# The last down projection of a hybrid decoder layer: half of its operand tiles for all tokens, the other half for two groups of 256 tokens

## The chip, the cores and the metric

The kernel runs on one core of one Trainium2 chip. Its time is the device time of one execution in microseconds (us); lower is better. One core has a matrix engine (TensorE, PE in the profile), a vector engine (VectorE, DVE), a scalar engine (ScalarE, ACT), a general engine (GpSimd, POOL) and a queue for transfers (SyncE, SP). They run side by side, each through its own list of instructions in order, and wait for each other by semaphores. Data lies in SBUF (128 partitions); matrix products arrive in PSUM, in banks of 512 float32 per partition.

## What is computed

One decoder layer over 16 meta tokens and 512 tokens, model width 2048: a norm, an input projection, a short convolution beside a recurrent group, an output projection with residual, then the part that matters here, a norm, a squared-ReLU MLP with residual, and the final norm:

```python
    h = rms_norm(h_res, norm_mlp_g[i])
    h_res = h_res + jnp.square(jax.nn.relu(h @ w_up[i])) @ w_down[i]
out = rms_norm(h_res, final_norm_g)          # over the 2048 features of a token
return out[:, N_META:]                       # 512 tokens x 2048, float32
```

`w_up` is 2048 x 8192, `w_down` 8192 x 2048.

## The kernel before

Everything is held feature by token: 2048 features are 16 tiles of 128 partitions (`KT` = 16), the 512 tokens (`SEQ`) are the columns. The MLP goes in 8 groups (`FFG`) of 1024 hidden features. In a group the **up stage** makes 8 tiles of hidden features (`UT` = 8; `u_hi`, `u_lo`), and the **down stage** makes 16 output tiles, each a sum over these 8 operand tiles, that are added to the residual `res`. Groups 0 to 6 are one loop; the last group is written out, since the final norm goes on in its down stage.

**Precision.** Each product is three matmuls in the type fp32r: high weight by high data, high by low, low by high (`dense`, the function with the matmuls at L1491). So one output tile over 8 operand tiles is 24 matmuls of 512 columns.

**Weights.** They come in quarters: four 128 x 128 blocks (256 KB) by one transfer that SP issues (`load`, L442) into one of 4 buffers `w_raw`. ACT makes the high part `w_hi` (`split`, L745) and DVE the low part `w_lo` (L1045), both in rings of 8 quarters. SP's next load into a buffer waits for DVE's `lo_split` of the quarter four earlier, ACT's split waits for the landing and for PE's use of the quarter eight earlier (`quarter_used`), DVE's split waits for ACT's (`hi_split`), and PE waits for `lo_split`. A down tile takes two quarters.

**PSUM.** Output tile n goes to one of two banks of `PD` by turns; PE begins tile n when tile n-2 has been taken out (`evacuated`). DVE takes a down tile out by adding it to `res` (L1397).

**The end of the last group**, output tile m by output tile m. DVE: add m, then two splits. ACT: multiply tile m of `res` by the final gain into `nt1` (L978, semaphore `gained`), two splits, and copy the turned tile m-1 from PSUM into `rows` (`keep_rows`, L987). PE: after the matmuls of tile m, turn tile m-1 to token by feature, four 128 x 128 transposes into `PW` (`turn_out`, L1760). POOL: square tile m of `res` into `psq` (L689) and add it into `acc` (L691), in a loop of two tiles per pass for tiles 0 to 13, tile 14 written out; DVE squares tile 15 itself (L1404). After the last tile PE sums the squares per token (L1775: for each of 4 blocks of 128 tokens a matmul with `acc` and one with `sq_last`, one column each), ACT takes the square root (L993), DVE the reciprocal (L1406), and ACT (L997) and DVE (L1410) scale each its half of the columns of `rows`, block by block; SP stores 8 pieces of 512 KB (L513).

Each engine's order is that of the code; nothing is reordered by a planner.

Of the kernel before, what the change touches and what calls it, by code (L numbers as in the profile page):

```python
# [31 lines left out]
P = 128  # L32
# [29 lines left out]
KQ = 4  # L62
# [130 lines left out]
T_END = T_MLP + FFG * 24  # L193
# [3 lines left out]
def hybrid_layer(nc, x, meta, norm_mix_g, w_in, shift_mu, conv_w, decay_w0, decay_w2, iclr_a0, iclr_a2,  # L197
# [224 lines left out]
    T_LAST = T_MLP + 24 * (FFG - 1) + UT  # L422

# [4 lines left out]
    def _(sp):  # L428
# [90 lines left out]
    def _(pool):  # L519
# [178 lines left out]
        squares(T_OUT, 0, False)  # L698
        squares(T_LAST, ACC_STEPS, True)
# [5 lines left out]
    def _(act):  # L705
# [246 lines left out]
        def mlp_group(g, last=False):  # L952
            n_split = [0]

            def splits(count):
                for _ in range(count):
                    if n_split[0] < 64 - (EDGE_LEAD + 4 if last else 0):
                        split(Q_MLP + EDGE_LEAD + 4 + n_split[0], 64, g)
                    n_split[0] += 1
# [13 lines left out]
            for m in range(KT):  # L973

                act.wait_ge(evacuated[(T_LAST + m) % 2], free(T_LAST + m))
                if m >= 3:
                    act.wait_ge(fin_turned, m - 2)
                nc.scalar.activation(nt1[:, m % 3, :], res[:, m, :], ACT.Copy, scale=p_("g_fin", m)).then_inc(gained, 1)  # L978
                splits(2)
                if m:  # L980
                    keep_rows(m - 1)
            keep_rows(KT - 1)

        def keep_rows(m):

            act.wait_ge(fin_turned, m + 1)
            nc.scalar.copy(rows[:, :, m * P:(m + 1) * P], PW[:, m % 4, :].rearrange("p (t n) -> p t n", t=4)).then_inc(fin_kept, 1)  # L987
# [4 lines left out]
        act.wait_ge(summed, 2)  # L992
        nc.scalar.activation(rs_tok[:], PW[:, 0, 0:4], ACT.Sqrt, bias=eps_t[:, 0:1], scale=1.0 / D).then_inc(rooted, 1)  # L993
        act.wait_ge(rs_ready, 2)
        for t in range(4):
            r = rows[:, t, DH:D]
            nc.scalar.activation(r, r, ACT.Copy, scale=rs_tok[:, t:t + 1]).then_inc(rows_scaled[1], 1)  # L997
# [3 lines left out]
    def _(dve):  # L1001
# [364 lines left out]
        def mlp_group(g, last=False):  # L1366
            n_split = [0]

            def splits(count):
                for _ in range(count):  # L1370
                    if n_split[0] < 64 - (EDGE_LEAD + 4 if last else 0):
# [17 lines left out]
            for m in range(UT):  # L1389
# [3 lines left out]
                splits(3)  # L1393
            for m in range(KT):
# [3 lines left out]
                splits(2)  # L1398
# [4 lines left out]
        dve.wait_ge(evacuated[(T_END - 1) % 2], free(T_END - 1))  # L1403
        V.tensor_tensor(sq_last[:], res[:, KT - 1, :], res[:, KT - 1, :], ALU.mult).then_inc(last_squared, 1)  # L1404
        dve.wait_ge(rooted, 2)
        V.reciprocal(rs_tok[:], rs_tok[:]).then_inc(rs_ready, 1)  # L1406
        dve.wait_ge(rs_ready, 2)
        dve.wait_ge(fin_kept, KT)
        for t in range(4):
            V.tensor_scalar(rows[:, t, 0:DH], rows[:, t, 0:DH], rs_tok[:, t:t + 1], None, ALU.mult).then_inc(rows_scaled[0], 1)  # L1410
# [3 lines left out]
    def _(pe):  # L1414
# [58 lines left out]
        def dense(tiles, ktiles, q0, n0, hi, lo, per_q=0, per_n=0, it=0, operand=None, one_bank=range(0), first=0, spare=0, cut=()):  # L1473
# [3 lines left out]
            for t in range(tiles):  # L1477
# [3 lines left out]
                for k in range(ktiles):  # L1481
# [6 lines left out]
                    for i, (w, v) in enumerate(((whi, hi), (whi, lo), (wlo, hi))):  # L1488
                        begin, end = (k == 0 and i == 0), (k == ktiles - 1 and i == 2)
                        if t in one_bank:  # L1490
                            ins = M(pd_seq(n), w, v[:, k, first:first + SEQ], start=begin, stop=end)  # L1491
# [262 lines left out]
        def turn_out(m):  # L1754

            pe.wait_ge(gained, m + 1)
            if m >= 4:
                pe.wait_ge(fin_kept, m - 3)
            for t in range(4):
                ins = nc.tensor.transpose(PW[:, m % 4, t * P:(t + 1) * P],  # L1760
                                          nt1[:, m % 3, t * P:(t + 1) * P], ident[:])
            ins.then_inc(fin_turned, 1)

        pe.wait_ge(rooted, 1)
        for i, _ in enumerate(down(FFG - 1), 1):
            if i % UT == 0 and i > UT:
                turn_out(i // UT - 2)

        pe.wait_ge(acc_step, 2 * ACC_STEPS)
        pe.wait_ge(fin_kept, KT - 3)  # L1770
        turn_out(KT - 1)
        pe.wait_ge(last_squared, 2)
        for t in range(4):
            for i, squares in enumerate((acc, sq_last)):
                ins = M(PW[:, 0, t:t + 1], squares[:, t * P:(t + 1) * P], ones[:, 0:1], start=(i == 0),  # L1775
                        stop=(i == 1))
        ins.then_inc(summed, 1)
# [29 lines left out]
```

## Time and profile before

| | |
|---|---|
| median of 3 runs | 2438.83 us (2438.52 to 2440.35) |
| profiled execution | 2439.01 us, of it span in the trace 2437.2 us |
| PE busy | 2406.8 us, 99% |
| DVE busy | 1129.1 us, 46% |
| ACT busy | 781.7 us, 32% |
| POOL busy | 193.8 us, 8% |
| down stage of the last group | 2324.0 to 2419.6 us of the span |
| from its last matmul to the end | 2419.6 to 2437.2 us |

The profiled execution stands 0.18 us over the median. Busy shares are means over the whole program; a stage is read from its own rows. "Idle before <-X" in a row is the time that the engine stood idle ahead of it, and what released it. The span is the time in the trace; 1.8 us of the device time lie outside it.

### The profile page before, as it was taken

The numbers are of one execution on the slowest core, as the hardware profiler recorded it, in microseconds if no ns is written. First come the engines' busy times: TensorE is split into PE (matmuls) and PEld (weight loads), VectorE is DVE, ScalarE is ACT, GpSimd is POOL, SyncE is SP. The second block draws the span as 40 slices with busy tenths as digits, with TensorE's granted clock in tenths as the row PEclk, the third lists the DMA queues.
The fourth block names the chain that finished last, engine by engine and source line by source line (L and its number), as shares of the span: only waits on it lengthen the run. The fifth ranks groups of instructions, "written<-read, shape, count | busy, mean of one in ns | idle before, by whom it ended". The sixth has DMA issues, their size and how long they took to land.

```text
span 2437.2 us, 42098 instructions
## 1 busy us (share of the span) xinstructions
PE 2406.8 (99%) x16524; PEld 2033.6 (83%) x16524; DVE 1129.1 (46%) x1733; ACT 781.7 (32%) x1321; POOL 193.8 (8%) x240
## 2 busy tenths in 40 slices
PE   8999999999999999999999999999999999999997
PEld 8999998999998788888888788888788887888886
DVE  7557657657657543533233333333333333333353
ACT  6533434434434322432232222221221322222333
POOL 5001101001001222000000000000000000000032
PEclk9999999999999999999999999999999999999998
DMA  8344244244244632333333233333332332333332
GB/s 246 81 98 102 69 100 98 71 102 99 73 104 108 192 103 82 100 98 93 87 104 95 81 110 94 88 97 94 87 104 87 91 108 79 104 98 91 89 99 92
DMA packets 487453, 243.65 MB, mean 100 GB/s; under 512 B 83295, under 2 KB 481121, under 8 KB 486881
## 3 DMA queue, kind: packets, MB, share of 16 engines
q1 hardware_dynamic: 480560, 222.62, 33.1%
q0 software_dynamic: 6720, 18.45, 2.4%
q8 instruction: 144, 2.36, 0.4%
q14 instruction: 29, 0.23, 0.0%
HBM read 224.08 MB, written 16.92 MB: 99 GB/s over the span
## 4 chain that ended last, share of the span: by engine, by line
PE 85%; DVE 9%; DMA 3%; ACT 1%; issue 1%; SPq 1%; ACTq 0%; DVEq 0%
PE PD L1491 66%; PE PD L1496 10%; PE PD L1705 2%; DVE w_lo L1045 1%; DVE uni L1140 1%; DVE uni L1266 1%; DMA w_raw<-in_w_in 1%; PE PD L1520 1%; PE PW L1520 1%; DMA UU<-gram 1%; DMA gram<-NA 1%; PE PW L1667 1%; PE PD L1425 0%; DVE uni L1144 0%; ACT w_hi L745 0%
## 5 line engine op out<-in xcount | busy, mean ns | idle before, releaser
L1045 DVE TENSOR_TENSOR w_lo<-w_raw,w_hi 128x512 fp32r<-128x512 f32 x780 | 544.2, 730 | 302.5 <-ACT w_hi L745 299.1
L745 ACT CAST w_hi<-w_raw 128x512 fp32r<-128x512 f32 x780 | 456.8, 618 | 702.7 <-PE PD L1491 519.9
L1491 PE MATMUL PD<-act_lo,w_hi 128*128 128x512 f32 x1344 | 531.3, 395 | 0.0
L1491 PE MATMUL PD<-act_hi,w_hi 128*128 128x512 f32 x1344 | 529.7, 394 | 1.5 <-DVE res L1338 1.5
L1491 PE MATMUL PD<-act_hi,w_lo 128*128 128x512 f32 x1344 | 528.7, 393 | 1.1 <-issue 1.1
L1491 PE MATMUL PD<-u_hi,w_hi 128*128 128x512 f32 x1024 | 409.7, 400 | 0.0
L1491 PE MATMUL PD<-u_hi,w_lo 128*128 128x512 f32 x1024 | 403.3, 394 | 0.0
L1491 PE MATMUL PD<-u_lo,w_hi 128*128 128x512 f32 x1024 | 401.5, 392 | 0.0
L1491 PEld LDWEIGHTS PD<-act_hi,w_hi 128*128 128x128 f32 x1344 | 252.4, 188 | 66.7 <-issue 4.8
L1491 PEld LDWEIGHTS PD<-act_hi,w_lo 128*128 128x128 f32 x1344 | 252.8, 188 | 57.2
L1491 PEld LDWEIGHTS PD<-act_lo,w_hi 128*128 128x128 f32 x1344 | 252.1, 188 | 58.0 <-issue 0.2
L1397 DVE TENSOR_TENSOR res<-PD,res 128x512 f32<-128x512 f32 x128 | 88.5, 692 | 407.7 <-PE PD L1491 407.7
L1496 PE MATMUL PD<-act_hi,w_hi 128*128 128x264 f32 (+1 forms) x1248 | 266.7, 295 | 0.0
L1496 PE MATMUL PD<-act_lo,w_hi 128*128 128x264 f32 (+1 forms) x1248 | 251.3, 283 | 0.0
L1496 PE MATMUL PD<-act_hi,w_lo 128*128 128x264 f32 (+1 forms) x1248 | 251.2, 283 | 0.0
L1491 PEld LDWEIGHTS PD<-u_hi,w_lo 128*128 128x128 f32 x1024 | 192.2, 188 | 49.9
L1491 PEld LDWEIGHTS PD<-u_lo,w_hi 128*128 128x128 f32 x1024 | 192.3, 188 | 45.4
L1491 PEld LDWEIGHTS PD<-u_hi,w_hi 128*128 128x128 f32 x1024 | 192.2, 188 | 43.6
L1381 DVE SCALAR_TENSOR_TENSOR nt<-PD,rs 128x512 f32<-128x512 f32 x64 | 44.3, 692 | 369.1 <-PE PD L1491 368.8
L965 ACT ACTIVATE nt<-nt 128x512 f32<-128x512 f32 x64 | 40.5, 633 | 515.6 <-DVE nt L1381 515.6
L1496 PEld LDWEIGHTS PD<-act_hi,w_hi 128*128 128x128 f32 x1248 | 192.6, 189 | 11.8 <-issue 6.7
L1496 PEld LDWEIGHTS PD<-act_hi,w_lo 128*128 128x128 f32 x1248 | 192.2, 188 | 0.0
(314 smaller groups left out, 1867.0 us busy)
## 6 DMA issues: line engine op xcount, KB each, us to landing
w_raw<-in_w_up SPq DMA_DIRECT2D x256, 256.0 KB, 3.2
w_raw<-in_w_down SPq DMA_DIRECT2D x256, 256.0 KB, 3.0
w_raw<-in_w_in SPq DMA_DIRECT2D x200, 256.0 KB, 3.2
w_raw<-in_w_out SPq DMA_DIRECT2D x64, 256.0 KB, 2.8
residual<-res POOLq DMA_DIRECT2D x2, 2048.0 KB, 9.9
out<-rows SPq DMA_DIRECT2D x8, 512.0 KB, 4.9
uni<-inverse SPq DMA_DIRECT2D x16, 240.0 KB, 4.0
yin<-mixed POOLq DMA_DIRECT2D x15, 256.0 KB, 3.8
```

Of the source, the lines that this page charges most:

```text
L745: nc.scalar.copy(w_hi[:, q % RING], w_raw[:, q % RAW]).then_inc(hi_split, 1)
L965: nc.scalar.activation(nt, nt, ACT.Square).then_inc(u_sq, 1)
L1045: V.tensor_tensor(w_lo[:, q % RING], w_raw[:, q % RAW], w_hi[:, q % RING].bitcast(F32), ALU.subtract).then_inc(lo_split, 1)
L1140: done("inv", V.reciprocal(fsq, fsq))
L1266: done("inv2", V.reciprocal(ysq, ysq))
L1381: V.scalar_tensor_tensor(nt1[:, m % 3, :], pd_seq(n), 0.0, rs1[:], ALU.max, ALU.mult).then_inc(evacuated[n % 2], 1)
L1397: V.tensor_tensor(res[:, m, :], pd_seq(n), res[:, m, :], ALU.add).then_inc(evacuated[n % 2], 1)
L1491: ins = M(pd_seq(n), w, v[:, k, first:first + SEQ], start=begin, stop=end)
L1496: ins = M(PD[:, 2 * (n % 2) + a, cols], w, v[:, k, start:start + cols.stop - cols.start], start=begin, stop=end)
L1520: ins = M(bank[:, h, cols], w, v[:, k, start:start + cols.stop - cols.start], start=begin, stop=end)
L1667: ins = M(PW[:, (c - 1) % 2, 0:P], GT[:, c - 1, :], HB[:, 0, :] if c == 1 else ZB[:, c - 2, :], start=True, stop=True)
L1705: ins = M(PD[:, OUT_BANK[t], :], w, v[:, k, 0:SEQ], start=(k == 0 and i == 0), stop=(k == KT - 1 and i == 2))
```

## The change

Only the down stage of the last group and what follows it. The first four operand tiles (the first quarter of each output tile) are multiplied for all 512 tokens, 16 output tiles of 12 matmuls with 512 columns, and added to `res` (**part one**). The last four operand tiles are multiplied for tokens 0 to 255, 16 tiles, and then for tokens 256 to 511, 16 tiles more (**part two**, 32 steps i = 0 to 31, 12 matmuls of 256 columns each). The quarters of part two are loaded and split once for each half. At every step of part two the gain, the turn (two transposes) and the copy to `rows` go over 256 tokens. At step 17 the squares of the first half are summed, rooted and inverted, at steps 19 and 20 its two blocks are scaled, and SP stores them. The same for the second half stands at the end. POOL's squares are written out, 15 tiles of 256 columns for each half, in part two only; DVE squares tile 15 of each half.

```diff
+        for m in range(KT):
+            load(wdn_q[FFG - 1, 0, :, :, m, :], Q_LAST + m)
+        for i in range(2 * KT):
+            load(wdn_q[FFG - 1, 1, :, :, i % KT, :], Q_HALF + i)
...
+        for h in range(2):                                   # POOL
+            cols = slice(h * NEAR, (h + 1) * NEAR)
+            for m in range(KT - 1):
+                n = T_HALF + h * KT + m
+                pool.wait_ge(evacuated[n % 2], free(n))
+                pool.wait_ge(acc_step, steps)
+                nc.gpsimd.tensor_tensor(psq[:, cols], res[:, m, cols], res[:, m, cols], ALU.mult).then_inc(acc_step, 1)
+                pool.wait_ge(acc_step, steps + 1)
+                nc.gpsimd.tensor_tensor(acc[:, cols], acc[:, cols], psq[:, cols], ALU.add).then_inc(acc_step, 1)
...
+            splits(KT)                                       # ACT
+            for i in range(2 * KT):
+                h, m = divmod(i, KT)
+                act.wait_ge(evacuated[(T_HALF + i) % 2], free(T_HALF + i))
+                if i >= 3:
+                    act.wait_ge(fin_turned, i - 2)
+                nc.scalar.activation(nt1[:, i % 3, 0:NEAR], res[:, m, h * NEAR:(h + 1) * NEAR], ACT.Copy,
+                                     scale=p_("g_fin", m)).then_inc(gained, 1)
+                splits(1)
+                if i:
+                    keep_rows(i - 1)
+                if i == SUM_AT:
+                    root_tokens(0)
+                if i in SCALE_AT:
+                    scale_rows(SCALE_AT.index(i))
...
             for m in range(KT):                              # DVE
-                n = T_MLP + UT + m
-                dve.wait_ge(quarter_used, at(Q_MLP + 4 * UT + 2 * (m + 1), 64, g))
+                n = T_LAST + m
+                dve.wait_ge(quarter_used, Q_LAST + m + 1)
                 V.tensor_tensor(res[:, m, :], pd_seq(n), res[:, m, :], ALU.add).then_inc(evacuated[n % 2], 1)
-                splits(2)
+                splits(1)
+            for i in range(2 * KT):
+                h, m = divmod(i, KT)
+                n, cols = T_HALF + i, slice(h * NEAR, (h + 1) * NEAR)
+                dve.wait_ge(quarter_used, Q_HALF + i + 1)
+                dve.wait_ge(evacuated[(T_LAST + m) % 2], free(T_LAST + m))
+                V.tensor_tensor(res[:, m, cols], pd_seq(n)[:, 0:NEAR], res[:, m, cols], ALU.add).then_inc(evacuated[n % 2], 1)
+                if m == KT - 1:
+                    dve.wait_ge(evacuated[n % 2], free(n))
+                    V.tensor_tensor(sq_last[:, cols], res[:, m, cols], res[:, m, cols], ALU.mult).then_inc(last_squared, 1)
+                splits(1)
+                if i == SUM_AT:
+                    invert_tokens(0)
+                if i in SCALE_AT:
+                    scale_rows(SCALE_AT.index(i))
...
+        for _ in dense(KT, KQ, Q_LAST, T_LAST, u_hi, u_lo, operand=operand, one_bank=range(KT)):   # PE
+            pass
+        pe.wait_ge(u_ready, UT * FFG)
+        for h in range(2):
+            near = dense(KT, KQ, Q_HALF + KT * h, T_HALF + KT * h, u_hi[:, KQ:UT], u_lo[:, KQ:UT], first=h * NEAR, width=NEAR,
+                         one_bank=range(KT))
+            for step_, _ in enumerate(near, 1):
+                i = KT * h + step_ // KQ - 1
+                if step_ % KQ == 0 and i:
+                    turn_out(i - 1)
+                if step_ % KQ == 0 and i == SUM_AT:
+                    sum_tokens(0)
+
+        turn_out(2 * KT - 1)
+        sum_tokens(1)
```

`splits` in the last group now covers 72 quarters after the first 8 instead of 56: 32 in the up stage, 16 in part one, one at each of the steps 0 to 23 of part two.

How instructions stand in a row, first on DVE where the up stage goes over into the down stage, before:

```order
L1381 SCALAR_TENSOR_TENSOR nt<-PD,rs 128x512 [waits u_ready,quarter_used]
L1045 TENSOR_TENSOR w_lo<-w_raw,w_hi 128x512 [waits hi_split]
L1386 TENSOR_TENSOR u_lo<-nt,u_hi 128x512 [waits u_hi_ready]
L1045 TENSOR_TENSOR w_lo<-w_raw,w_hi 128x512 [waits hi_split] x3
L1397 TENSOR_TENSOR res<-PD,res 128x512 [waits quarter_used]
L1045 TENSOR_TENSOR w_lo<-w_raw,w_hi 128x512 [waits hi_split] x2
```

and in the changed kernel on DVE where part one goes over into part two (L1442 is the add of part one, L1449 that of part two, L1083 the split):

```order
L1442 TENSOR_TENSOR res<-PD,res 128x512 [waits quarter_used]
L1083 TENSOR_TENSOR w_lo<-w_raw,w_hi 128x512 [waits hi_split]
L1449 TENSOR_TENSOR res<-PD,res 128x256 [waits evacuated1,quarter_used]
L1083 TENSOR_TENSOR w_lo<-w_raw,w_hi 128x512 [waits hi_split]
L1449 TENSOR_TENSOR res<-PD,res 128x256 [waits evacuated0,quarter_used]
```

A tile had two splits behind its add; now every add of 256 columns has one split behind it and one ahead.

ACT in the last group's down stage before (`nt1` is the gained tile, `rows` the copy of the turned one):

```order
L987 COPY rows<-PW 128x4x128 [waits fin_turned]
L978 ACTIVATE nt1<-res,par 128x512 [waits fin_turned,evacuated1]
L745 CAST w_hi<-w_raw 128x512 [waits quarter_used,raw_loaded0]
L745 CAST w_hi<-w_raw 128x512 [waits quarter_used,raw_loaded1]
L987 COPY rows<-PW 128x4x128 [waits fin_turned]
```

and in part two of the changed kernel:

```order
L1001 ACTIVATE nt1<-res,par 128x256 [waits fin_turned,evacuated1]
L767 CAST w_hi<-w_raw 128x512 [waits quarter_used,raw_loaded0]
L1016 COPY rows<-PW 128x2x128 [waits fin_turned]
L1001 ACTIVATE nt1<-res,par 128x256 [waits fin_turned,evacuated0]
L767 CAST w_hi<-w_raw 128x512 [waits quarter_used,raw_loaded1]
```

The gain still stands ahead of the split, at half the width; the split has its full width, and there is one for each gain.

POOL where the squares of the last group begin, before (ISA and REGISTER_ALU rows are waits and address arithmetic of the loop):

```order
L683 MEMSET acc 128x512 [waits summed]
L693 UNCONDITIONAL_BRANCH
L693 ISA
L688 ISA [waits evacuated1]
L689 ISA [waits acc_step]
L689 TENSOR_TENSOR psq<-res 128x512
L690 REGISTER_ALU
L691 TENSOR_TENSOR acc<-acc,psq 128x512 [waits acc_step]
```

and in the changed kernel:

```order
L710 MEMSET acc 128x512 [waits summed]
L718 TENSOR_TENSOR psq<-res 128x256 [waits acc_step,evacuated1]
L720 TENSOR_TENSOR acc<-acc,psq 128x256 [waits acc_step]
L718 TENSOR_TENSOR psq<-res 128x256 [waits acc_step,evacuated0]
L720 TENSOR_TENSOR acc<-acc,psq 128x256 [waits acc_step]
```

The loop and its arithmetic are gone, and the pair of operations comes 30 times at half the width.

## Rows read from the trace of the kernel before

**Rows 1.** The page's first part: busy time, share, instructions.
```profile
PE 2406.8 (99%) x16524; PEld 2033.6 (83%) x16524; DVE 1129.1 (46%) x1733; ACT 781.7 (32%) x1321; POOL 193.8 (8%) x240
```
**Rows 2.** Chain that ended last, from 2380 us: start, length, what.
```profile
2413.55 0.44 PE PW L1760 x4
2413.99 5.61 PE PD L1491 x24
...
2419.62 0.70 DVE res L1397
...
2420.35 0.73 ACT nt L978
...
2421.33 0.63 PE PW L1760 x4
2421.95 1.78 PE PW L1775 x16
```
**Rows 3.** Timeline, DVE, up stage into down stage: start, length, line, idle before.
```profile
2323.96 0.69 DVE L1381 SCALAR_TENSOR_TENSOR nt<-PD,rs 128x512 f32<-128x512 f32 x1 [5.46 <-PE PD L1491]
...
2327.73 1.89 DVE L1045 TENSOR_TENSOR w_lo<-w_raw,w_hi 128x512 fp32r<-128x512 f32 x3
2329.56 0.69 DVE L1397 TENSOR_TENSOR res<-PD,res 128x512 f32<-128x512 f32 x1
...
2337.15 2.39 DVE L1045 TENSOR_TENSOR w_lo<-w_raw,w_hi 128x512 fp32r<-128x512 f32 x2 [1.30 <-ACT w_hi L745]
```
**Rows 4.** Timeline, ACT, one output tile of the last down stage.
```profile
2335.88 0.72 ACT L978 ACTIVATE nt<-res,par 128x512 f32<-128x512 f32 x1 [3.40 <-DVE res L1397]
2336.51 1.12 ACT L745 CAST w_hi<-w_raw 128x512 fp32r<-128x512 f32 x2
```
**Rows 5.** Timeline, PE, pairs of 260 and 256 columns: first and last of 26.
```profile
599.89 0.40 PE L1496 MATMUL PD<-act_hi,w_hi 128*128 128x260 f32 x2
...
605.84 0.40 PE L1496 MATMUL PD<-act_lo,w_hi 128*128 128x260 f32 x2
```
**Rows 6.** Timelines, DVE and then POOL, at three output tiles of the last stage.
```profile
2349.22 0.69 DVE L1045 TENSOR_TENSOR w_lo<-w_raw,w_hi 128x512 fp32r<-128x512 f32 x1 [1.30 <-ACT w_hi L745]
2349.83 1.78 DVE L1045 TENSOR_TENSOR w_lo<-w_raw,w_hi 128x512 fp32r<-128x512 f32 x1
...
2413.59 0.69 DVE L1397 TENSOR_TENSOR res<-PD,res 128x512 f32<-128x512 f32 x1 [5.34 <-PE PD L1491]
...
2336.12 1.04 POOL L689 TENSOR_TENSOR psq<-res 128x512 f32 x1 [2.66 <-DVE res L1397]
...
2349.30 1.75 POOL L691 TENSOR_TENSOR acc<-acc,psq 128x512 f32<-128x512 f32 x1
...
2414.36 1.04 POOL L689 TENSOR_TENSOR psq<-res 128x512 f32<-128x512 f32 x1 [3.44 <-DVE res L1397]
2415.48 1.29 POOL L691 TENSOR_TENSOR acc<-acc,psq 128x512 f32<-128x512 f32 x1
```
**Rows 7.** Groups by form (count, busy us, mean ns), then the scaling's timeline.
```profile
L1016 DVE COPY res<-PD 128x256 f32<-128x256 f32 x1 | 0.4, 425 | 4.2 <-PE PD L1446 4.2
...
L563 POOL TENSOR_TENSOR centre<-ident,head_mean 128x128 f32<-128x128 f32 x1 | 0.5, 458 | 0.1
...
2424.27 4.27 ACT L997 ACTIVATE rows<-rows,rs_tok 128x1024 f32<-128x1024 f32 x4 [0.24 <-DVE rs_tok L1406]
2424.27 2.74 DVE L1410 TENSOR_SCALAR rows<-rows,rs_tok 128x1024 f32<-128x1024 f32 x4
```
**Rows 8.** Windows in the last stores: five engines' busy time, granted clock, DMA share, GB/s.
```profile
2426.00:2426.50 0.50, 0.00 (x0) 0.00 (x0) 0.50 (x2) 0.50 (x2) 0.00 (x0) 0.50 1.02 410
...
2436.00:2436.50 0.50, 0.00 (x0) 0.00 (x0) 0.00 (x0) 0.00 (x0) 0.00 (x0) 0.50 0.58 221
```
**Rows 9.** Windows with the granted clock: near the program's start, and in its tail.
```profile
19.50:21.00 1.50, 0.57 (x5) 0.60 (x6) 0.84 (x3) 1.50 (x5) 0.21 (x2) 1.00 0.16 26
...
2423.00:2423.50 0.50, 0.50 (x6) 0.50 (x5) 0.00 (x0) 0.00 (x0) 0.00 (x0) 0.91 0.00 0
```

More of the change, by code:

```diff
@@ L420, in hybrid_layer @@
     RS_CUT = META + 3 * P
-    T_LAST = T_MLP + 24 * (FFG - 1) + UT
     block = ctx.enter_context(nc.Block())
@@ L956, in splits @@
                 for _ in range(count):
-                    if n_split[0] < 64 - (EDGE_LEAD + 4 if last else 0):
+                    if n_split[0] < (80 - EDGE_LEAD - 4 if last else 64):
                         split(Q_MLP + EDGE_LEAD + 4 + n_split[0], 64, g)
@@ L991, in _ @@
         mlp_group(FFG - 1, last=True)
[L992 to L997, printed above, removed]
+        root_tokens(1)
+        for t in range(2, 4):
+            scale_rows(t)
     @block.vector
@@ L1370, in splits @@
                 for _ in range(count):
-                    if n_split[0] < 64 - (EDGE_LEAD + 4 if last else 0):
+                    if n_split[0] < (80 - EDGE_LEAD - 4 if last else 64):
                         split(Q_MLP + EDGE_LEAD + 4 + n_split[0], 64, g)
@@ L1393, in mlp_group, with invert_tokens, scale_rows @@
                 splits(3)
+            if not last:
+                for m in range(KT):
+                    n = T_MLP + UT + m
+                    dve.wait_ge(quarter_used, at(Q_MLP + 4 * UT + 2 * (m + 1), 64, g))
+                    V.tensor_tensor(res[:, m, :], pd_seq(n), res[:, m, :], ALU.add).then_inc(evacuated[n % 2], 1)
+                    splits(2)
+                return
             for m in range(KT):
-                n = T_MLP + UT + m
-                dve.wait_ge(quarter_used, at(Q_MLP + 4 * UT + 2 * (m + 1), 64, g))
+                n = T_LAST + m
+                dve.wait_ge(quarter_used, Q_LAST + m + 1)
                 V.tensor_tensor(res[:, m, :], pd_seq(n), res[:, m, :], ALU.add).then_inc(evacuated[n % 2], 1)
-                splits(2)
+                splits(1)
+            for i in range(2 * KT):
+                h, m = divmod(i, KT)
+                n, cols = T_HALF + i, slice(h * NEAR, (h + 1) * NEAR)
[10 more added lines that the diff above has]
+                    scale_rows(SCALE_AT.index(i))
+        def invert_tokens(h):
+            dve.wait_ge(rooted, 2 + h)
+            r = rs_tok[:, 2 * h:2 * h + 2]
+            V.reciprocal(r, r).then_inc(rs_ready, 1)
+        def scale_rows(t):
+            dve.wait_ge(rs_ready, 2 + t // 2)
+            dve.wait_ge(fin_kept, KT * (t // 2 + 1))
+            V.tensor_scalar(rows[:, t, 0:DH], rows[:, t, 0:DH], rs_tok[:, t:t + 1], None, ALU.mult).then_inc(rows_scaled[0], 1)
         with dve.Fori(0, FFG - 1) as g:
@@ L1402, in _ @@
         mlp_group(FFG - 1, last=True)
[L1403 to L1410, printed above, removed]
+        invert_tokens(1)
+        for t in range(2, 4):
+            scale_rows(t)
     @block.tensor
@@ L1490, in dense @@
                         if t in one_bank:
-                            ins = M(pd_seq(n), w, v[:, k, first:first + SEQ], start=begin, stop=end)
+                            ins = M(pd_seq(n)[:, 0:width], w, v[:, k, first:first + width], start=begin, stop=end)
                             continue
@@ L1769, in _, with turn_out @@
[L1769 to L1777, printed above, removed]
+        def turn_out(i):
+            pe.wait_ge(gained, i + 1)
+            if i >= 4:
+                pe.wait_ge(fin_kept, i - 3)
+            for t in range(2):
+                ins = nc.tensor.transpose(PW[:, i % 4, t * P:(t + 1) * P],
+                                          nt1[:, i % 3, t * P:(t + 1) * P], ident[:])
+            ins.then_inc(fin_turned, 1)
@@ new lines, in sum_tokens @@
+        def sum_tokens(h):
+            pe.wait_ge(acc_step, ACC_STEPS + 1 + 2 * (KT - 1) * (h + 1))
+            pe.wait_ge(last_squared, 2 + h)
+            for t in range(2):
+                for i, squares in enumerate((acc, sq_last)):
+                    ins = M(PD[:, 1 + 2 * h, t:t + 1], squares[:, (2 * h + t) * P:(2 * h + t + 1) * P], ones[:, 0:1],
+                            start=(i == 0), stop=(i == 1))
+            ins.then_inc(summed, 1)
+        pe.wait_ge(rooted, 1)
+        operand = lambda k: pe.wait_ge(u_ready, UT * (FFG - 1) + k + 1)
```

61 lines of the change are left out of this document (32 added, 29 removed).

## The prediction, made before the changed kernel ran

> **What bounds the kernel now.** The page's first part says it: PE is busy 99% of the span, DVE and ACT are not [rows 1]. So time is won only where PE's work gets less or where PE has nothing to do. The chain that ended last shows both [rows 2]: in the last down stage 5.61 us of 24 matmuls (0.2335 us each) and 0.44 us of four transposes by turns, with nothing between; then from 2419.62, the end of the last matmul, 17.6 us to the end of the span at 2437.2 in which PE does almost nothing. The change goes for that tail. It pays in the stage ahead of it, where adds, gains, turns and splits, spread over 6.04 us per tile so far, have to fit into steps of about a quarter of that. So the timelines of DVE, ACT and POOL come next [rows 3, 4, 6]: what follows what, and how soon.
>
> **Part one.** The stage begins at 2323.96, where DVE takes out the last up tile [rows 3]. 16 tiles of 12 matmuls at 0.2335 are 44.8 us. One stall: the first add is due after 2.8 us, at 2326.8, but DVE stands in its splits until 2329.56 [rows 3]; tile 2 needs that bank, could start at 2329.56 and has it at 2330.25. That is 0.7 us. Afterwards an add (0.69) and a split (0.60, from the start spacing of three in 1.89 [rows 3]) fit into 2.8. Part two begins at 2323.96 + 44.8 + 0.7 = 2369.5.
>
> **Part two, PE's own work.** Pairs of 260 and 256 columns, each matmul with its weight load, start 5.95 us apart for 25 pairs [rows 5], 0.238 a pair, so 0.119 for 258 columns and 0.118 for 256: 1.42 us a step. The narrow matmuls cost next to nothing extra (1.42 against 1.40 for half of a 512-column tile of this depth). Two transposes are 0.22. If PE stayed the bound, part two would take 32 x 1.42 + 30 x 0.22 + 0.9 for the sum of the first half (8 of the 16 small matmuls that took 1.78 [rows 2]) = 52.9.
>
> **Part two, the ring of waits.** It doesn't stay the bound. At steps 0 to 23 the order tables show: DVE adds tile i, then splits a quarter, and that split waits for ACT's split of the same quarter; ACT makes its gain of tile i first, and that waits for DVE's add. So add i, gain i, high split, low split, add i+1 stand in one row. That ACT or DVE has idle time does not help, and PE can't run ahead by more than two banks. In numbers, from the start of an add:
> - add of 256 columns: 0.43, from 0.69 for 512 and the PSUM copies of DVE, 0.425 at 256 [rows 3, 7].
> - gain: starts 0.03 later [rows 2]. At 512 columns the split behind it starts 0.63 later [rows 4]; at 1024 columns such an operation repeats every (4.27 - 1.14)/3 = 1.04, with one of them at 1.14 long [rows 7], so 0.8 ns a column and 0.42 at 256. ACT's split starts at 0.88.
> - DVE's low split can start 0.64 after ACT's (2336.51 to 2337.15 [rows 3, 4]), at 1.52, and takes 0.60 to the next add: **2.13 us**, if nothing else is in the way.
>
> **And POOL is in the way.** It works at each step from 0 to 14 and 16 to 30 now. The rows show what that costs [rows 6]: with POOL's add into acc running from 2349.30 to 2351.05, DVE's second split lasts 1.78 in place of 0.69 and ends 0.56 after POOL's does; POOL's add took 1.75 in place of 1.29. POOL's own times: square 1.04 and add 1.29 at 512 columns alone, starting 0.08 after DVE's add (2414.28 to 2414.36) and 0.08 after each other [rows 6]; 0.458 at 128 columns [rows 7] gives a slope of 2.2 ns and 0.18 fixed, so 0.74 for the add at 256 and 0.61 for the square. From the start of DVE's add: square 0.51 to 1.12, add 1.20 to 1.94. DVE's split wants to start at 1.52, ends at 1.94 + 0.56 = 2.50, and the next add starts 0.08 earlier, since DVE's operations overlap by that much: **2.42 us** a step. I take this one, because POOL's add starts 0.32 before DVE asks. The bounds are 2.13 (DVE first, POOL after it) and 2.61 (POOL starts 0.27 after DVE's add ends, as in the loop before: ACT's gain starts at 2335.88, so the add ended at 2335.85, and POOL starts at 2336.12 [rows 4, 6]; the loop's arithmetic is gone now).
>
> The Trainium skill, page "SBUF — State Buffer", section "SBUF: two separate sides", says that VectorE with two SBUF inputs and a reading GpSimd operation exclude each other, the first one holding the port for its whole instruction. The trace agrees with it: 1.78, and an end 0.56 after POOL's. If they shared a rate instead (1.09 us lost in 1.22 us side by side), the 0.42 us of overlap here would cost 0.37, a step 2.50, and the sum below would come out 1.8 us higher.
>
> **The sum of part two.** Add 0 starts at 2369.5 + 1.42 + 0.02 = 2370.9. To add 23 there are 23 steps: 22 x 2.42, and step 15 with no POOL work at 2.13 (DVE's extra square of tile 15 hides while it waits for ACT), together 55.4. Step 17 adds 0.2 for the reciprocal (ACT's root is done by then: it comes at 1.7 to 2.0 in a step of 2.42). Steps 19 and 20 add DVE's scaling, 0.69 each [rows 7], since it stands between split and add; ACT's, 1.04, ends before its next gain. Together 57.0: add 23 at 2427.9. From step 24 there are no splits left and PE binds again. It still waits for gain 23 (0.98 after add 23) and 0.25 to start (2421.08, where the last gain ends, to 2421.33 [rows 2]), turns (0.22), does tile 25; the same once more behind gain 24; then five steps of 1.64: add 31 starts 2.42 + 0.98 + 0.25 + 0.22 + 1.42 + 5 x 1.64 = 13.5 later, at 2441.4. Before, the last add started at 2419.62: **21.8 us later**.
>
> **The tail.** Before, from the last add to the scaling 4.65 (2419.62 to 2424.27). After: add 0.43, gain 0.03 + 0.52, start 0.25, two transposes 0.32, sums 0.89, root and reciprocal 0.54 as before: 2.98, 1.67 less. POOL's last add ends 0.3 us after add 31 starts, under it. The stores then bind: 8 pieces, 4.19 MB, keep the transfers full from 2426.0 to 2436.3 at some 405 GB/s [rows 8]; four pieces take 5.15 instead of 10.3. ACT's second block is scaled 2.2 after the first begins, ahead of its transfer. Together the tail is **6.8 us shorter**.
>
> **Costs taken at nothing.** 16 more loads: SP's load for step i is released four steps (over 9 us) ahead, against about 3 us to land; cover is gone only if steps fall under 1 us. The stores of the first half stand behind all loads in SP's list, but the last load is released at step 19 and the first block is scaled there, so they run under steps 20 to 27. ACT's own work in a step (0.42 + 0.52 + 0.3) is 1.3, below the ring.
>
> **Total.** +21.8 - 6.8 = +15.0 on the profiled execution's 2439.0, so 2454.0; the median stands 0.2 lower: **2453.8 us**.
>
> **Rivals.**
> - *Ring without POOL* (12%): DVE's split gets in first. 22 x 0.29 less: 2447.4. For it: only 0.32 us decide, and POOL's times at 256 columns are estimates. Against: whoever asks first holds, and POOL asks first.
> - *Ring stretched* (6%): POOL starts late as in the loop, or overlap is shared: 2.50 to 2.61, 2455.6 to 2458.
> - *PE stays the bound, not slower* (3%): 52.9 for part two, add 31 at 2422.4, 2.8 later, less 6.8: 2434.8, just within 0.2%. It needs a ring below 1.64, and the change stops paying from a ring of about 1.77 on (15.0 / 23 below 2.42). The four links alone, with no semaphore between, are 0.43 + 0.42 + 0.62 + 0.60 = 2.07, so it would take a step of the ring that isn't one.
> - *The clock falls* (5%): in part two PE would stand idle 0.8 of 2.42 us. At 1.2 GHz, half of the granted 2.4, a step is 3.28 and PE binds: part two 106, up to 2488. Against: near the start PE was busy for 0.57 of 1.5 us at a granted clock of 1.00 [rows 9]; it fell to half only in the tail, where from 2420.0 on PE had stood idle 1.3 us and then did one-column matmuls (0.91 in the window of the change [rows 9]).
> - *The early stores don't run early* (2%): 5.15 more, 2459.
>
> **How the numbers follow.** The forecast (ring with POOL, 2450 to 2457) gets 72%, the rivals 12, 6, 3, 5 and 2. Range 2446 to 2460: it takes in both bounds of the ring, and 1 to 2 us for tail and transitions. A measurement here can tell about 0.2%, 4.9 us. Faster by more than that 0.01 (even the ideal gains 4.0), within it 0.04, slower 0.95.
>
> **What would show it.** In the trace of the changed kernel: adds of 256 columns 2.4 us apart at steps 0 to 14, about 2.1 at step 15, 3.1 at 19 and 20, 1.64 from step 26; DVE's splits lasting 0.9 to 1.0 beside POOL's add, and idle before "ACT w_hi"; PE idle 0.8 us in each step, waiting for the gain; part one 45.5 us; the last add near 2441, and 10.8 us from there to the end. Wrong it would be if adds were 1.64 apart (the ring isn't closed), 2.13 (no POOL in it) or 3.3 (the clock).

## The result, and the profile after

The changed kernel takes 2452.23 us (median of 5 runs, 2450.43 to 2453.43) against 2438.52 for the one before (5 runs beside them, 2438.14 to 2440.35): a ratio of 1.0057, interval 1.0046 to 1.0068. It is slower by 13.7 us; 15.0 were forecast (2453.8).

Both kernels do the same work up to the last down stage, but they reach it at different times: the last up tile is scaled at 2323.96 before [rows 3] and at 2323.17 after, and in the kernels of the experiments below anywhere from 2319.64 to 2323.69, although nothing ahead of it was changed in any of them. So the traces are compared below by the **stretch** from the start of that scaling to the end of the span: 113.24 us before, 127.33 after, 14.1 more. Each kernel was traced once, but the stretch repeats where kernels should not differ: the last add starts 116.87 us after the scaling here and in experiment 6, and 116.86 in experiment 5 with the added work outside the ring.

The first part of the page after, to be held against [rows 1]:

```profile
span 2450.5 us, 42509 instructions
PE 2413.4 (98%) x16716; PEld 2045.7 (83%) x16716; DVE 1146.0 (47%) x1783; ACT 797.8 (33%) x1370; POOL 195.1 (8%) x270
```

The timeline of DVE after (start us, us, engine, line, operation, out<-in, shape, count, idle before and what ended it). It answers to [rows 3] and [rows 6]:

```profile
2323.17 0.69 DVE L1419 SCALAR_TENSOR_TENSOR nt<-PD,rs 128x512 f32<-128x512 f32 x1 [5.45 <-PE PD L1555]
...
2370.43 0.43 DVE L1449 TENSOR_TENSOR res<-PD,res 128x256 f32<-128x256 f32 x1
2371.94 0.97 DVE L1083 TENSOR_TENSOR w_lo<-w_raw,w_hi 128x512 fp32r<-128x512 f32 x1 [1.09 <-ACT w_hi L767]
2372.84 0.41 DVE L1449 TENSOR_TENSOR res<-PD,res 128x256 f32<-128x256 f32 x1
2374.34 0.97 DVE L1083 TENSOR_TENSOR w_lo<-w_raw,w_hi 128x512 fp32r<-128x512 f32 x1 [1.08 <-ACT w_hi L767]
2375.23 0.41 DVE L1449 TENSOR_TENSOR res<-PD,res 128x256 f32<-128x256 f32 x1
...
2407.75 0.69 DVE L1083 TENSOR_TENSOR w_lo<-w_raw,w_hi 128x512 fp32r<-128x512 f32 x1 [0.63 <-ACT w_hi L767]
...
2415.59 0.41 DVE L1449 TENSOR_TENSOR res<-PD,res 128x256 f32<-128x256 f32 x1
2417.09 0.97 DVE L1083 TENSOR_TENSOR w_lo<-w_raw,w_hi 128x512 fp32r<-128x512 f32 x1 [1.08 <-ACT w_hi L767]
2417.98 0.74 DVE L1467 TENSOR_SCALAR rows<-rows,rs_tok 128x1024 f32<-128x1024 f32 x1
2418.64 0.41 DVE L1449 TENSOR_TENSOR res<-PD,res 128x256 f32<-128x256 f32 x1
```

And of ACT, and of POOL, in the same steps:

```profile
2373.29 0.51 ACT L1001 ACTIVATE nt<-res,par 128x256 f32<-128x256 f32 x1 [1.38 <-DVE res L1449]
2373.70 0.60 ACT L767 CAST w_hi<-w_raw 128x512 fp32r<-128x512 f32 x1
2374.21 0.36 ACT L1016 COPY rows<-PW 128x256 f32<-128x256 f32 x1
```

```profile
2373.33 0.61 POOL L718 TENSOR_TENSOR psq<-res 128x256 f32<-128x256 f32 x1 [0.96 <-DVE res L1449]
2374.02 0.73 POOL L720 TENSOR_TENSOR acc<-acc,psq 128x256 f32<-128x256 f32 x1
```

The ring of waits can be read off in one step, by start times: DVE's add 2372.84, ACT's gain 2373.29, ACT's high split 2373.70, DVE's low split 2374.34, next add 2375.23, which is 2.39 us after the first. POOL's add ends at 2374.75, and DVE's split, which began its record at 2374.34, ends 0.56 later and lasts 0.97. The split at 2407.75 is the control within the same trace: it stands in step 15, where POOL has no square or add, and it takes 0.69.

The waits between 2371 and 2428 (engine and line, what it waited for: us in total, times, longest):

```profile
ACT nt L1001 <- DVE res L1449: 25.6, 24, 1.4
DVE w_lo L1083 <- ACT w_hi L767: 25.6, 24, 1.1
...
PE PW L1824 <- ACT nt L1001: 12.1, 22, 1.2
```

DVE waits for ACT and ACT for DVE, the same 25.6 us each, and PE waits behind both: 0.55 us on average, 0.51 in a plain step and 1.17 and 1.18 behind the two scalings. After such a wait the two transposes last 0.44 us in place of 0.22, so a plain step loses 0.73 us against PE's own 1.655. The last steps and the tail, in the chain that ended last (start us, us, what; against [rows 2]):

```profile
2430.30 1.44 PE PD L1555 x12
2431.74 0.22 PE PW L1824 x2
...
2440.04 0.44 DVE res L1449
2440.48 0.02 issue
2440.50 0.52 ACT nt L1001
2441.02 0.04 issue
2441.06 0.44 PE PW L1824 x2
2441.50 0.80 PE PD L1833 x8
2442.30 0.02 issue
2442.32 0.27 ACT rs_tok L1021
2442.59 0.02 issue
2442.62 0.18 DVE rs_tok L1462
```

Three windows (stretch, its length, busy us and count of PE, PEld, DVE, ACT and POOL, granted clock, DMA share, GB/s):

```profile
2372.00:2384.00 12.00, 9.58 (x74) 8.56 (x73) 6.58 (x11) 6.32 (x15) 6.80 (x11) 1.00 0.38 109
2420.00:2422.00 2.00, 1.52 (x13) 1.32 (x12) 1.87 (x3) 1.42 (x3) 0.55 (x1) 1.00 1.07 417
2444.00:2448.00 4.00, 0.00 (x0) 0.00 (x0) 0.23 (x1) 1.01 (x1) 0.00 (x0) 0.50 0.91 364
```

The clock stayed at 1.00, its 2.4 GHz level, through the ring; the first half's rows are stored from 2420 on, under the second half's work (417 GB/s in the first two microseconds, the last load of weights among it); and the last four pieces leave in the tail.

### The profile page after: what moved, and what is told of

It reads as the page before. It is cut to its first block, busy times and chain, and to the rows that moved or that the text cites. A ratio compares the mean times of both kernels' runs of the same rounds, so it can differ in the third digit from the quotient of the medians.

```text
span 2450.5 us, 42509 instructions
## 1 busy us (share of the span) xinstructions
PE 2413.4 (98%) x16716; PEld 2045.7 (83%) x16716; DVE 1146.0 (47%) x1783; ACT 797.8 (33%) x1370; POOL 195.1 (8%) x270
## 3 DMA queue, kind: packets, MB, share of 16 engines
q8 instruction: 146, 2.39, 0.4%
## 4 chain that ended last, share of the span: by engine, by line
PE 86%; DVE 8%; issue 2%; ACT 2%; DMA 1%; SPq 0%; ACTq 0%; DVEq 0%
PE PD L1555 65%; PE PD L1560 12%; PE PD L1769 2%; DVE w_lo L1083 1%; DVE uni L1178 1%; DVE uni L1304 1%; PE PD L1584 1%; ACT w_hi L767 1%; PE PW L1584 1%; PE PW L1731 1%; DVE res L1449 0%; PE PD L1489 0%; DVE uni L1182 0%; PE PW L1695 0%; PE PW L1633 0%
## 5 line engine op out<-in xcount | busy, mean ns | idle before, releaser
L767 ACT CAST w_hi<-w_raw 128x512 fp32r<-128x512 f32 x796 | 468.0, 619 | 734.5 <-PE PD L1555 549.1
L1083 DVE TENSOR_TENSOR w_lo<-w_raw,w_hi 128x512 fp32r<-128x512 f32 x796 | 549.6, 721 | 314.1 <-ACT w_hi L767 310.5
L1555 PE MATMUL PD<-u_hi,w_hi 128*128 128x512 f32 (+1 forms) x1088 | 421.8, 388 | 0.8 <-DVE res L1442 0.8
L1555 PE MATMUL PD<-u_hi,w_lo 128*128 128x512 f32 (+1 forms) x1088 | 414.2, 381 | 0.0
L1555 PE MATMUL PD<-u_lo,w_hi 128*128 128x512 f32 (+1 forms) x1088 | 412.3, 379 | 0.0
L1436 DVE TENSOR_TENSOR res<-PD,res 128x512 f32<-128x512 f32 x112 | 77.5, 692 | 371.3 <-PE PD L1555 371.3
L1555 PEld LDWEIGHTS PD<-u_hi,w_lo 128*128 128x128 f32 x1088 | 204.2, 188 | 46.9
L1555 PEld LDWEIGHTS PD<-u_lo,w_hi 128*128 128x128 f32 x1088 | 204.6, 188 | 42.9
L1555 PEld LDWEIGHTS PD<-u_hi,w_hi 128*128 128x128 f32 x1088 | 204.3, 188 | 42.8 <-DVE res L1442 1.2
```

The source lines that it names most:

```text
L767: nc.scalar.copy(w_hi[:, q % RING], w_raw[:, q % RAW]).then_inc(hi_split, 1)
L1083: V.tensor_tensor(w_lo[:, q % RING], w_raw[:, q % RAW], w_hi[:, q % RING].bitcast(F32), ALU.subtract).then_inc(lo_split, 1)
L1555: ins = M(pd_seq(n)[:, 0:width], w, v[:, k, first:first + width], start=begin, stop=end)
```

## The experiments

The theory: the ring (add, gain, high split, low split) sets the step, and POOL's two operations lengthen its last link, because DVE's split does not run beside them. Its rivals: POOL does not matter; the length of ACT's work does, wherever it stands; it is not the order of operations but their amount. All edits below are made to the changed kernel and touch part two alone, if nothing else is said.

**1. The split ahead of the gain.** ACT's split needs nothing of this step's add; only the order of the lines puts it behind.

```diff
+                splits(1)
                 act.wait_ge(evacuated[(T_HALF + i) % 2], free(T_HALF + i))
...
                 nc.scalar.activation(nt1[:, i % 3, 0:NEAR], ...)
-                splits(1)
```

> The changed kernel with one edit: at each step of part two ACT makes the high split ahead of the gain, so the split waits for the matmuls of tile i and no longer for DVE's add. Theory (a ring add, gain, high split, low split): the ring is cut, steps 0 to 23 fall from 2.39 us toward PE's own 1.65, and 24 x 0.74 = 17.8 us come off at most. POOL (1.43 us a step) and DVE's split (0.6) then ask for the same time, 2.0 in 1.65, so POOL falls behind by 0.35 a step and the sums of each half wait 2 to 3 us for it: about 2439, between 2436 and 2442. Rival (steps are long because 256-column matmuls or the doubled loads are slow): the step stays near 2.39, time near 2452.

2438.47 us (10 runs), before beside it 2437.67 (19 runs), ratio 1.0003, interval 0.9994 to 1.0013: the whole loss is gone. The stretch is 113.3. So the ring was the loss, and ACT and DVE have the time for their work. But the shorter tail doesn't show as a gain either: the last add starts 102.47 after the scaling, 6.8 later than in the kernel before, and the tail is 6.8 shorter. Of the 6.8, 4.4 are there without POOL's work too (experiment 4: PE's narrow matmuls and the first half's sums, the stall in part one, two waits for a gain). The timelines of this kernel say where the rest went. DVE:

```profile
2371.58 0.96 DVE L1083 TENSOR_TENSOR w_lo<-w_raw,w_hi 128x512 fp32r<-128x512 f32 x1 [0.28 <-ACT w_hi L767]
...
2397.42 0.41 DVE L1449 TENSOR_TENSOR res<-PD,res 128x256 f32<-128x256 f32 x1
```

and POOL:

```profile
2372.08 1.07 POOL L720 TENSOR_TENSOR acc<-acc,psq 128x256 f32<-128x256 f32 x1
...
2394.99 0.88 POOL L718 TENSOR_TENSOR psq<-res 128x256 f32<-128x256 f32 x1
2395.94 1.01 POOL L720 TENSOR_TENSOR acc<-acc,psq 128x256 f32<-128x256 f32 x1
2397.09 0.88 POOL L718 TENSOR_TENSOR psq<-res 128x256 f32<-128x256 f32 x1
```

and its waits:

```profile
PE PD L1833 <- POOL acc L720: 2.1, 1, 2.1
```

POOL has no idle time ahead of any of these rows. Its pair (0.61 + 0.73) comes every 1.57 us where DVE has no split left, just under PE's 1.65 a step; beside DVE's splits it comes every 1.98 us on average over the first half's 15 pairs (2.10 in the rows shown), and POOL is the slowest engine. It falls behind, and PE waits 2.1 us for the first half's sums at step 17. In the chain that ended last POOL stands from 2391.0 to the end of its adds at 2427.6, where PE forms the last sums; that end costs 0.35 (10.82 from the last add to the end against 10.47 in experiment 4). DVE's adds are not touched: the one at 2397.42 lies wholly inside POOL's square (2397.09 to 2397.97) and takes 0.41. It has one operand in PSUM, the split has both in SBUF.

**2. POOL idle.** Its square and add in part two become one-column fills, with the same semaphores; the final norm lacks these squares.

```diff
-                nc.gpsimd.tensor_tensor(psq[:, cols], res[:, m, cols], res[:, m, cols], ALU.mult).then_inc(acc_step, 1)
+                nc.gpsimd.memset(psq[:, 0:1], 0.0).then_inc(acc_step, 1)
...
-                nc.gpsimd.tensor_tensor(acc[:, cols], acc[:, cols], psq[:, cols], ALU.add).then_inc(acc_step, 1)
+                nc.gpsimd.memset(psq[:, 0:1], 0.0).then_inc(acc_step, 1)
```

> The changed kernel, but in part two POOL's squares and adds are each replaced by a one-column memset (the final norm then lacks these squares). Order and semaphores stay. Theory: DVE's split no longer waits for POOL, it lasts 0.69 in place of 0.97, and the step falls from 2.39 to the four links alone, 2.11 to 2.13: 21 x 0.27 = 5.7 us less, about 2446.5. Rival (POOL's share is nothing, the split is long for another reason): step stays 2.39, 2452.

2446.4 us in one run, stretch 121.0, which is 6.3 less than after. Its timeline of DVE:

```profile
2373.08 0.42 DVE L1449 TENSOR_TENSOR res<-PD,res 128x256 f32<-128x256 f32 x1
2374.58 0.69 DVE L1083 TENSOR_TENSOR w_lo<-w_raw,w_hi 128x512 fp32r<-128x512 f32 x1 [1.09 <-ACT w_hi L767]
2375.19 0.42 DVE L1449 TENSOR_TENSOR res<-PD,res 128x256 f32<-128x256 f32 x1
```

The split is asked for at the same point of the step (1.50 after the add) and takes 0.69; the step is 2.11. POOL's part of the step is 0.28, the other links are 2.11.

**3. POOL busy with fills.** Is it POOL's activity, or what its operations do? First two fills of 512 columns for the square and the add (again without those squares), then three.

```diff
-                nc.gpsimd.tensor_tensor(psq[:, cols], res[:, m, cols], res[:, m, cols], ALU.mult).then_inc(acc_step, 1)
+                nc.gpsimd.memset(psq[:], 0.0).then_inc(acc_step, 1)
...
-                nc.gpsimd.tensor_tensor(acc[:, cols], acc[:, cols], psq[:, cols], ALU.add).then_inc(acc_step, 1)
+                nc.gpsimd.memset(psq[:], 0.0).then_inc(acc_step, 1)
```

> The changed kernel, but in part two POOL's two operations are memsets of 512 columns (0.53 us each in the trace of before): POOL is as busy at the time of DVE's split, 1.2 to 1.7 us into a step, and writes SBUF, but reads nothing (the final norm then lacks these squares). Theory that DVE's two-source split and POOL exclude each other by their reads: step 2.11 to 2.13 as with POOL idle, about 2446.5. Rival (any work of POOL on SBUF holds DVE up): split of 0.8 to 0.9, step 2.2 to 2.4, 2448 to 2452.

2442.8 us in one run; the stretch is 121.0 as with POOL idle (the time is lower because this execution reached the stage 3.6 us earlier). But the run decides little: the second fill ran from 2374.75 to 2375.27 and DVE's split started at 2375.20, so they were side by side for 0.07 us only. Hence a third fill, ahead of the last:

```diff
+                nc.gpsimd.memset(act_lo[:, m, :].bitcast(mybir.dt.float32), 0.0)
                 nc.gpsimd.memset(psq[:], 0.0).then_inc(acc_step, 1)
```

> GpSimd's square and add of each step of the last four operand tiles are replaced by three fills of 512 columns each (0.52 us each beside the gaps of 0.06 in the earlier run with two fills), so that GpSimd is at work from about 0.48 to 2.2 us after the start of VectorE's add, over the whole of VectorE's weight split (asked for at 1.50, 0.69 long). The final norm lacks these squares. Theory A, only GpSimd's operations on two tensors shut VectorE's split out: the step stays at 2.11 us and the split at 0.69, and from the last scaling to the end of the span 121.0 us pass, as with two fills. Rival B, any work of GpSimd on its memory port shuts VectorE's split out: the split ends some 0.56 us behind the last fill, that is at 2.8 rather than 2.19, the step grows to about 2.7 us (0.6 more, over 24 steps), and the stretch to about 135 us.

2445.06 us in one run, stretch 121.25. Its rows of DVE and of POOL:

```profile
2375.07 0.69 DVE L1084 TENSOR_TENSOR w_lo<-w_raw,w_hi 128x512 fp32r<-128x512 f32 x1 [1.08 <-ACT w_hi L768]
...
2377.18 0.69 DVE L1084 TENSOR_TENSOR w_lo<-w_raw,w_hi 128x512 fp32r<-128x512 f32 x1 [1.09 <-ACT w_hi L768]
```

```profile
2374.62 0.54 POOL L720 MEMSET act_lo<- 128x528 f32 x1
2375.10 0.53 POOL L721 MEMSET psq<- 128x512 f32 x1
```

Now the fill from 2375.10 to 2375.63 lies wholly inside the split from 2375.07 to 2375.76, and neither is longer than alone; steps stay 2.11 apart. The stretch is 0.2 longer than in experiment 2 behind the last add alone; up to that add 110.54 and 110.52 us pass. So what shuts the split out is not POOL at work but its add, which unlike a fill reads SBUF.

**4. The first two together**: split first and POOL idle, to see what the change is worth where nothing binds but PE.

> Both edits: split ahead of the gain, and POOL's squares in part two replaced by one-column memsets (the final norm lacks these squares). Theory: PE binds all of part two at 1.65 a step, part two takes 53 us, and the time is what the prediction gave for PE as the bound, 2434.8, about 4 below the kernel before. Rival (something else holds a step over 1.65, such as landings of the doubled loads, or PSUM's two banks): steps of 1.8 and more, 2438 or above.

2434.73 us (10 runs), ratio 0.999, interval 0.9981 to 1.0. The stretch is 110.6, 2.7 below before, adds 1.65 apart. This is what the forecast's third rival, "PE stays the bound", described, and it is near its price: 2.7 by the stretch (2.9 by the medians) in place of 4.0. The rows of DVE show steps in which DVE waits for PE, with all doubled loads and narrow matmuls in place, so neither of these sets the step:

```profile
2373.34 0.42 DVE L1449 TENSOR_TENSOR res<-PD,res 128x256 f32<-128x256 f32 x1 [0.25 <-PE PD L1555]
...
2374.99 0.42 DVE L1449 TENSOR_TENSOR res<-PD,res 128x256 f32<-128x256 f32 x1 [0.26 <-PE PD L1555]
```

**5. More work of ACT inside the ring, and outside it.** A second gain of 256 columns into a buffer that nobody reads: between gain and split, or behind the copy of the rows.

```diff
                 nc.scalar.activation(nt1[:, i % 3, 0:NEAR], ...)
+                nc.scalar.activation(act_lo[:, m, h * NEAR:(h + 1) * NEAR], res[:, m, h * NEAR:(h + 1) * NEAR], ACT.Copy, scale=p_("g_fin", m))
                 splits(1)
                 if i:
                     keep_rows(i - 1)
```

> The changed kernel with one more ACT operation of 256 columns at each step of part two (the gain once more, into a place that nobody reads), between gain and split. Theory (ring of four links, POOL's add beside it): ACT's split comes 0.42 later, DVE's split asks at 1.92 instead of 1.50, when POOL's add (it ends 1.93 after the add's start) is over, so the step is the bare ring plus 0.42 = 2.53, 0.14 over 2.39, and DVE's split lasts 0.69 again. From the last up tile's scaling to the end 127.3 + 23 x 0.14 = 130.5. If POOL had no part in the step: 2.39 + 0.42 = 2.81, 137. If the ring isn't what binds: 127.3.

> The same extra ACT operation, but behind the copy to rows, so outside the ring. Theory: ACT has 1.1 us free in a step of 2.39, the step stays 2.39, and the stretch from the last up tile's scaling to the end stays 127.3. Rival (ACT is simply too full): step 2.39 + 0.42, 137.

Inside: one run, 2453.84 us, stretch 130.57, adds 2.51 apart:

```profile
2371.32 0.42 DVE L1450 TENSOR_TENSOR res<-PD,res 128x256 f32<-128x256 f32 x1
2373.22 0.69 DVE L1084 TENSOR_TENSOR w_lo<-w_raw,w_hi 128x512 fp32r<-128x512 f32 x1 [1.48 <-ACT w_hi L767]
2373.83 0.42 DVE L1450 TENSOR_TENSOR res<-PD,res 128x256 f32<-128x256 f32 x1
```

The operation delays the split by 0.40, and the step grows only by 0.12: DVE now asks at 1.90, just as POOL's add ends, and its split is back at 0.69. That is the ring of the forecast's lower bound, DVE's split untouched by POOL, with 0.40 more in it, and one run sizes the two terms (0.40 more of ACT, 0.28 less of POOL). Outside: one run, 2449.94 us, stretch 127.3, steps of 2.39, nothing. The same work costs 3.2 us or none by its place in the list.

**6. The stores held back.** SP waits for three scaled blocks before it stores the first.

```diff
-                sp.wait_ge(rows_scaled[h], t + 1)
+                sp.wait_ge(rows_scaled[h], max(t + 1, 3))
```

> The changed kernel, with one edit: SP waits with the stores of the first half until the first block of the second half is scaled, so all eight pieces leave at the end. Theory (the last 10.46 us are short because only four pieces of 512 KB are left): the stretch up to the last add stays 116.9, and the tail grows by four pieces at some 405 GB/s, 5.2 us, to 15.6; from the last up tile's scaling to the end 132.5. Rival (the tail is shorter because of sums and scaling, the stores overlap anyway): 127.3 to 129.

2454.68 us in one run, stretch 132.6. The last add starts 116.87 after the scaling, exactly as in the changed kernel, and from there to the end it takes 15.72 in place of 10.46: 5.26 more, for the four pieces that were put at 5.15. Transfers run at 404 to 406 GB/s from 2442 to 2452. So the early stores bring what was reckoned, and cost the work that they run under nothing that shows.

**7. A version without ring and without POOL's squares.** The split goes first, and DVE makes each square right behind its add (0.42 us, of which it has enough), so that POOL only adds.

```diff
+                    V.tensor_tensor(squares_of[:, m, cols], res[:, m, cols], res[:, m, cols], ALU.mult).then_inc(squared, 1)
...
-                nc.gpsimd.tensor_tensor(psq[:, cols], res[:, m, cols], res[:, m, cols], ALU.mult).then_inc(acc_step, 1)
-                pool.wait_ge(acc_step, steps + 1)
-                nc.gpsimd.tensor_tensor(acc[:, cols], acc[:, cols], psq[:, cols], ALU.add).then_inc(acc_step, 1)
+                pool.wait_ge(squared, KT * h + m + 1 - h)
+                nc.gpsimd.tensor_tensor(acc[:, cols], acc[:, cols], squares_of[:, m, cols], ALU.add).then_inc(acc_step, 1)
```

> Split ahead of the gain, and DVE makes the squares of all tiles of part two right behind its adds (each into a place of its own), POOL only adds them up, 0.73 a step instead of 1.43. Theory: DVE's two-source work and POOL's add then fit into 1.65 (0.35 + 0.61 + 0.73 = 1.69, with slack in DVE's order), PE binds, and the whole result costs what the kernel with an idle POOL took: 2434.7, 3 below the kernel before, 4 below split-first with POOL's squares. Rival (any sharing of the port costs the ring): over 2437.

2434.49 us (10 runs), before beside it 2436.3 (21 runs), ratio 0.9994, interval 0.9985 to 1.0003; stretch 111.06. Steps are 1.65. What is left are the starts of the stage and of the row scaling:

```profile
2399.80 0.68 DVE L1086 TENSOR_TENSOR w_lo<-w_raw,w_hi 128x512 fp32r<-128x512 f32 x1
2400.41 1.23 DVE L1472 TENSOR_SCALAR rows<-rows,rs_tok 128x1024 f32<-128x1024 f32 x1
2401.56 0.41 DVE L1452 TENSOR_TENSOR res<-PD,res 128x256 f32<-128x256 f32 x1
```

Beside POOL's add the scaling takes 1.23 us in place of 0.74, and the next adds come 2.55 rather than 1.65 apart, twice. (POOL's add runs from 2400.05 to 2401.08 there: the scaling ends 0.56 later, like every blocked split.) So in the last version the first half is scaled at steps 24 and 26, where no split is left, its sum comes one step later, and the last up tile's three splits go behind the first add of part one, which removes that part's stall.

```diff
-SUM_AT, SCALE_AT = KT + 1, (KT + 3, KT + 4)
+SUM_AT, SCALE_AT = KT + 2, (KT + 8, KT + 10)
...
-                splits(3)
+                if not last or m < UT - 1:
+                    splits(3)
...
-                splits(1)
+                splits(4 if m == 0 else 1)
```

> As the one before, with two more edits: the first half's sums stand at step 18 and its two scalings at steps 24 and 26, where no splits are left; and the last up tile's last three low splits stand behind the first add of part one instead of ahead of it. Theory: the first takes 1.1 us of waiting of PE for ACT's gain at steps 20 to 22 away, the second the 0.7 us at the start of part one: 2434.7 - 1.8 = 2432.9, ratio 0.998 to the kernel before. Rival (the early stores at step 24 and later collide with the last ones): no gain over the one before, 2434.7.

2432.54 us (11 runs, 2431.57 to 2434.26) against 2436.3, ratio 0.9985, interval 0.9976 to 0.9994: faster than the kernel before by 3.8 us, and the fastest of the study, though less than the 0.2% that one comparison here can safely tell. By the traces the stretch is 108.66, 4.6 less than before. Against the version before it the stretch is 2.4 shorter, where 1.8 was expected. The two edits were not run apart, but the trace parts them: the first add of part two starts 46.28 after the scaling in place of 47.26 (0.98 less), and the other 1.4 come off between that add and the last one, 51.94 us in place of 53.36. From 2320 us on, its chain that ended last has little but PE in it ahead of the final stores (shares by engine and line):

```profile
by line: PE PD L1561 84.0%; PE PW L1830 6.3%; ACTq L1861 1.9%; PE PD L1839 1.4%; ACT nt L1005 0.5%; DVE res L1453 0.4%; ACT rs_tok L1024 0.2%; issue 0.2%; DVE rs_tok L1468 0.2%; ACT rows L1031 0.0%
```

## Why the prediction was right

- **Part one**, 46.9 us from the scaling to add 0: measured 47.26. The stall came as said (PE idle 0.76 before tile 2); of the 0.3 missing, 0.16 is the last matmul's run-out, its record lasting 0.28 where the spacing of 0.12 was counted; the rest is spread over the starts.
- **PE's own step**, 1.64: measured 1.655 (1.44 + 0.22), on 30 steps 0.45 us.
- **The ring**, 2.42: measured 2.39. The links were 0.45 (add to gain), 0.41 (gain to split), 0.64 (high to low split) and 0.89. POOL's add started 1.18 after DVE's (1.20 expected) and DVE asked at 1.50 (1.52), so the order of the two, the choice on which 6 us hung, held at every step; the blocked split ended 0.56 after POOL's add, as in [rows 6]. That the two engines don't share a rate but one is shut out for the other's whole instruction (the Trainium skill, page "SBUF — State Buffer", section "SBUF: two separate sides") agrees with these rows too: with 0.41 us side by side, a shared rate was priced at a step of 2.50, and 2.39 was seen, with POOL's add at its 0.73 of working alone. The same section of the Trainium skill limits this to GpSimd operations that read SBUF, and the fills of experiment 3, which read nothing, agree.
- **Step 15** 2.11 (2.13 expected); **steps 19 and 20** 3.05 each (3.11). **Step 17** grew by 0.08, not 0.2: the reciprocal overlaps the next add. Add 0 to add 23 took 56.04 (57.0), add 23 to add 31 13.57 (13.5). From the scaling to the last add 116.87, before 95.66 by [rows 2, 3]: 21.2 later, 21.8 forecast. The steps from add 0 to add 23 gave 1.0 less than forecast, the way to add 0 0.3 more and the last eight steps 0.1 more.
- **The tail** took 10.46 from the last add, before 17.58: 7.1 shorter (6.8 forecast). The term that was off is PE's start behind the last gain, put at 0.25 and 0.04 long, with the transposes at 0.44 where 0.32 stood; the sums took 0.80, not 0.89. The stores' term, 5.15, measured 5.26 in experiment 6.
- **The clock** stayed at 1.00 through a ring in which PE stood idle 0.51 us of each 2.39. The forecast had put that idle time at 0.8; the loss per step was 0.73, of which 0.22 show as longer transposes.
- **Sum**: +21.2 and -7.1 are +14.1 on the stretch; with an execution that reached the stage 0.8 earlier, 13.3 between the spans and 13.7 between the medians.
- **"PE stays the bound"** was priced at 4.0 below before; experiment 4 gave 2.7. Its steps were 1.655 (0.3 us over the 23), and PE waited 1.2 us for gains behind the scaling of the rows. The last version of experiment 7, without those, has 4.6, of which 0.98 was won ahead of part two's first add.
- **What the prediction didn't see** is that the ring hid a second limit. With it gone, POOL's pair, every 1.57 us by itself, slows to 1.98 beside DVE's splits and binds. The forecast didn't depend on it; its sentence that the change stops paying at a ring of 1.77 did: with POOL's squares in place, a ring of 1.65 pays nothing (experiment 1).

## What to carry to other kernels

When a stage is cut into smaller tiles, write out each engine's list for one step as start times and look for a closed ring: here two engines, each busy for little more than half of the step (6.58 and 6.32 of 12 us), waited for each other through one line that stood behind a wait it didn't need. Here, moving that line ahead of the wait took back 14.0 us of the stretch, and taking away nearly all of POOL's work 6.3. The engine that was second slowest has to be counted at its speed beside the others, not alone. Between VectorE and GpSimd, count a VectorE operation with both operands in SBUF and a GpSimd operation that reads SBUF as exclusive; VectorE's adds with one operand in PSUM, and GpSimd's fills, ran free here.

## What the runs showed of the hardware

- DVE's scaling of 1024 columns, one tensor and one number per row, takes 0.74 us alone and 1.23 beside POOL's add (experiment 7): an operation needn't read two tensors to be held up. At 0.74 for 1024 columns it is about twice as fast a column as the adds (0.69 for 512). The section "SBUF: two separate sides" of the page "SBUF — State Buffer" of the Trainium skill names VectorE operations in a two-port mode beside those with two inputs; the trace doesn't say which mode this one ran in.
- It works both ways: POOL's add of 256 columns takes 0.73 alone and 1.07 beside DVE's split of 2371.58, its square 0.61 and 0.88 (experiment 1). The 1.01 at 2395.94 stands beside DVE's square of tile 15 (2395.92, 0.43), whose two operands are one and the same tile. DVE's add out of PSUM is not held up (0.41 to 0.43 with POOL at work all the time).
- POOL's fill of 512 columns takes 0.53 wholly inside DVE's split of 0.69, and neither gets longer (experiment 3).
- The same code ahead of the stage ended up to 4.3 us apart in the profiled executions (2319.64 to 2323.96), and 21 single times of the kernel before lay between 2433.7 and 2438.9 on one chip. A difference of a few us between single times needs a stretch like the one used here.
